# Eight of twelve modulation pieces moved from TensorE to ScalarE and GpSimd, with both layers written out

## The reference, cut to what matters

```python
for l in range(2):
    mod = einsum('bd,dk->bk', silu(c), w_ada[l]) + b_ada[l]          # 1024 x 6144 weights
    shift1, scale1, gate1, shift2, scale2, gate2 = split(mod, 6)
    h = rms_norm(x, norm1_g[l]) * (1 + scale1) + shift1
    proj = h @ w_in[l]                          # c_q 256, c_kv 128, k_rope 64, conv_u 1024
    attn_out = mla_group(...)                   # 4 heads, 512 x 512 scores
    conv_out = conv_group(conv_u, ...)          # gate, depthwise conv of 31 taps, norm, silu
    x = x + gate1 * (concat(attn_out, conv_out) @ w_out[l])
    h2 = rms_norm(x, norm2_g[l]) * (1 + scale2) + shift2
    x = x + gate2 * expert_choice_ffn(h2, ...)  # 16 experts, 64 tokens each, 12.6 MB of weights each
```

## Time and profile before

| | |
|---|---|
| median of three runs | 2568.12 us (2565.55 to 2569.09) |
| the profiled execution's own time | 2573.45 us |
| its span, first to last instruction | 2571.7 us |
| mean granted TensorE clock | 0.97 |
| TensorE busy | 2371.3 us, 92% |
| VectorE, ScalarE, GpSimd busy | 1126.1, 912.9, 268.7 us |
| layer 0, layer 1 start at (line 538) | 21.1, 795.6 us |
| key diagonal (line 1217) of layer 0, 1 | 161.3, 929.3 us |
| second block starts at about | 1558 us |

### The profile page before, as it was taken

One profiled execution on the slowest core, in us unless ns is written; L12 is line 12 of the kernel. 1 busy time (PEld: TensorE's weight loads), 2 busy tenths in 40 slices (PEclk: granted clock), 3 DMA queues, 4 the chain that ended last, 5 costly groups with the idle time before them and its releaser, 6 DMA issues. The chain is left out here.

```text
span 2571.7 us, 31324 instructions
## 1 busy us (share of the span) xinstructions
PE 2371.3 (92%) x12693; PEld 1495.2 (58%) x12693; DVE 1126.1 (44%) x1688; ACT 912.9 (35%) x1228; POOL 268.7 (10%) x245
## 2 busy tenths in 40 slices
PE   6998799998987999799999988999999999989997
PEld 5744544333335834534333437887888777767776
DVE  4976312211214975312111225647611112458997
ACT  4247211111114246211111116656632234247775
POOL 0000100000000000100000005000255433300100
PEclk8989899999998989899999999999999999989999
DMA  9801579999999601489999995422223421159995
GB/s 343 290 1 38 225 320 429 429 428 429 428 425 338 231 1 61 201 358 428 428 428 429 428 420 164 164 82 86 78 78 99 135 69 62 50 188 376 370 367 212
DMA packets 202868, 650.48 MB, mean 253 GB/s; under 512 B 12144, under 2 KB 110718, under 8 KB 177918
## 3 DMA queue, kind: packets, MB, share of 16 engines
q1 hardware_dynamic: 199028, 637.98, 63.7%
q0 software_dynamic: 2592, 7.87, 0.8%
q10 hardware_dynamic: 1130, 2.99, 0.3%
HBM read 641.99 MB, written 8.39 MB: 253 GB/s over the span
## 5 line engine op out<-in xcount | busy, mean ns | idle before, releaser
L847 PE MATMUL ps<-ring,hy 128*64 128x512 f32 x992 | 225.0, 595 | 37.1 <-DMA ring<-in_w_up 26.1
L1354 DVE TENSOR_TENSOR scr<-scr,ps 128x512 f32<-128x512 f32 x32 | 22.0, 688 | 504.2 <-PE ps L847 504.2
L847 PE MATMUL ps<-ring,scr 128*64 128x512 f32 x992 | 224.5, 594 | 16.8 <-DMA ring<-in_w_up 14.7
L1621 POOL TENSOR_TENSOR raw_r<-raw,w_high 128x512 fp32r<-128x512 f32 (+1 forms) x160 | 189.7, 1219 | 433.5 <-ACT w_high L1889 433.5
L874 PE MATMUL ps<-ring,scr 128*64 128x512 f32 x1024 | 227.2, 595 | 3.1 <-ACT scr L1064 2.7
L1644 PE MATMUL ps<-x_high,w_high 128*128 128x512 f32 x464 | 186.4, 402 | 3.6 <-DVE y L2285 3.6
L1646 PE MATMUL ps<-x_high,raw_r 128*128 128x512 f32 x464 | 184.5, 398 | 0.0
L1645 PE MATMUL ps<-xT_r,w_high 128*128 128x512 f32 x464 | 183.1, 395 | 0.0
L2710 DVE TENSOR_TENSOR ring_r<-ring,ring_high 128x2048 fp32r<-128x2048 f32 x77 | 172.8, 2285 | 22.0 <-ACT ring_high L2633 22.0
L847 PEld LDWEIGHTS ps<-ring,hy 128*64 128x64 f32 x992 | 68.4, 137 | 188.7 <-issue 123.4
L1141 DVE SCALAR_TENSOR_TENSOR one_hot_T<-h_tok,convw,one_hot_T 128x512 f32<-128x512 f32 x240 | 166.5, 749 | 1.8
(11 more groups left out here) (594 smaller groups left out, 4547.5 us busy)
## 6 DMA issues: line engine op xcount, KB each, us to landing
ring<-in_w_up SPq DMA_DIRECT2D x64, 2048.0 KB, 25.6
ring<-in_w_down SPq DMA_DIRECT2D x64, 2048.0 KB, 20.4
ring<-in_w_gate SPq DMA_DIRECT2D x60, 2048.0 KB, 23.0
ring<-in_w_up SPq DMA_DIRECT2D x56, 1024.0 KB, 6.9
ring<-in_w_ada SPq DMA_DIRECT2D x22, 2048.0 KB, 13.5
ring<-in_w_down SPq DMA_DIRECT2D x28, 1024.0 KB, 7.0
raw<-in_w_in SPq DMA_DIRECT2D x24, 1024.0 KB, 5.1
raw<-in_w_in SPq DMA_DIRECT2D x20, 512.0 KB, 5.2
```

What stands on the lines that cost most here:

```text
L847: mm = pe.matmul(ps[CAP * half:CAP * (half + 1), 1 + j // 2, :], x_e[j % 2][:, at_x:at_x + CAP], weights[:, k, half * HALF:(half + 1) * HA ...
L1621: part = pool.tensor_tensor(dst[:, a:a + 2], src[:, a:a + 2], high[:, a:a + 2].bitcast(F32), ALU.subtract)
```

## The change

- Pieces 5 to 12 (numbers 4 to 11) no longer go through TensorE's `ada_chunk`. Of the eight row tiles of a piece ScalarE scales the first four by the conditioning vector (`ada_scale`), GpSimd the other four; GpSimd then adds 2048, 1024 and 512 columns, and TensorE sums the 128 partitions of the result with four products of two columns (`ada_sums`). The pieces are taken in the order 6, 7, 8, 9, 4, 5, 10, 11. Loads of the later pieces and of the output weights wait for GpSimd's `ada_made`.
- The first four pieces are cut by rows (two row tiles, 2048 columns: runs of 8 KB), and go into four banks together.
- Both layers are written out; the branches on `l` become Python's.
- The 40 small products stand between the head products, their evacuation (`rbias`, `xmod`) behind the rotary parts.
- Taps: 68 behind tiles, 29 around the heads, 27 in attention. The convolution's mean, variance and normalization come three, three and two steps later.
- In the first pair of experts the first half is turned before the second half's gather ends, and the second half's turn and the gates come behind the first weight chunk.

Its core:

```diff
-TAPS_IN_TILE = (0, 5, 9, 9, 10, 10, 10, 10, 6, 1, 5, 4)
-TAPS_IN_HEADS = (16, 8)
-TAPS_IN_STEP = (3, 3, 2, 4, 3, 4, 2)
+TAPS_IN_TILE = (0, 5, 7, 8, 8, 8, 8, 8, 7, 1, 4, 4)
+TAPS_IN_HEADS = (20, 9)
+TAPS_IN_STEP = (3, 3, 3, 3, 3, 3, 3, 3, 3)
...
-ADA_PLACES = (0, 1, 2, 3, 0, 1, 2, 0, 1, 2, 0, 1)
+ADA_PLACES = (0, 1, 2, 3, 0, 1, 2, 1, 0, 1, 0, 1)
+ADA_CHUNK = (6, 7, 8, 9, 4, 5, 10, 11)
...
-    sp.dma_start(ada_place(M, c), w_ada[:, :, HALF * c:HALF * (c + 1)]).then_inc(ahead["ada"][c], 16)
+    sp.dma_start(first_rows(M, c), w_ada[:, 2 * c:2 * c + 2, 0:4 * HALF]).then_inc(ahead["ada"][c], 16)
+
+
+def first_rows(M, c):
+
+    return ada_place(M, c).rearrange("p k n -> p (k n)").rearrange("p (k n) -> p k n", k=2)
...
+    spare = ring[:, 2 * CHUNK - HALF:2 * CHUNK]
+    ada_acc = [spare, one_hot_T[:, 3 * KT * P:3 * KT * P + HALF]] * 2 + [spare, scr[:, 2, :], scr[:, 1, :], scr[:, 2, :]]
+    SUM_AT = [(6, 2 * P + 8 * k) for k in range(4)] + [(7, 2 * GROUP), (7, 2 * GROUP + 8), (7, 0), (7, 8)]
+    ada_row_all = one_hot_T[:, CHUNK:CHUNK + 4 * P].rearrange("p (c n) -> p c n", c=4)
...
                 before = max(b for b in range(c) if ADA_PLACES[b] == ADA_PLACES[c])
-                sp.wait_ge(ada_used, before + 1)
-                sp.dma_start(ada[c], w_ada[:, :, HALF * c:HALF * (c + 1)]).then_inc(ada_in[ADA_PLACES[c]], 16)
+                if before < 4:
+                    sp.wait_ge(ada_used, before + 1)
+                else:
+                    sp.wait_ge(ada_made, before - 3)
+                at_column = HALF * ADA_CHUNK[c - 4]
+                sp.dma_start(ada[c], w_ada[:, :, at_column:at_column + HALF]).then_inc(ada_in[ADA_PLACES[c]], 16)
...
-            for piece, then in ((2, (5,)), (CT, (6,)), (3, range(7, 12))):
+            for piece, then in ((2, (5,)), (CT, (6,)), (3, (7, 8))):
...
-            sp.wait_ge(ada_used, 12)
+            sp.wait_ge(ada_made, 3)
...
+            for c in range(9, 12):
+                ada_chunk(c)
             w = at("w_out").rearrange("a (k p) n -> p (a k) n", p=P)
             for k in range(0, KT, 4):
-                sp.dma_start(w_out[:, k:k + 4], w[:, k:k + 4]).then_inc(w_out_in, 16)
+                sp.wait_ge(ada_made, 7 + k // 4)
+                sp.dma_start(w_out[:, k:k + 4], w[:, k:k + 4]).then_inc(w_out_in[k // 4], 16)
...
+            step = Steps(pool, ada_step)
+            c_col = M["c_col"]
+            for k, acc_k in enumerate(ada_acc):
+                piece = ada[4 + k]
+                pool.wait_ge(ada_in[ADA_PLACES[4 + k]], ada_landed(4 + k, l))
+                for kt in range(4, KT):
+                    step(pool.tensor_scalar(piece[:, kt, :], piece[:, kt, :], c_col[:, kt:kt + 1], None, ALU.mult))
+                step.settle()
+                pool.wait_ge(ada_rows, k + 2)
+                step(pool.tensor_tensor(piece[:, 0:4, :], piece[:, 0:4, :], piece[:, 4:8, :], ALU.add))
+                step.settle()
+                step(pool.tensor_tensor(piece[:, 0:2, :], piece[:, 0:2, :], piece[:, 2:4, :], ALU.add))
+                step.settle()
+                if 2 <= k <= 4:
+                    pool.wait_ge(ada_cols, 4 + k - 1)
+                if k == 5:
+                    pool.wait_ge(lat_ss, 3)
+                if k == 7:
+                    pool.wait_ge(ada_cols, 4 + 6)
+                pool.tensor_tensor(acc_k, piece[:, 0, :], piece[:, 1, :], ALU.add).then_inc(ada_made, 1)
+
...
-            def ada_chunk(c, bank):
+            def ada_sums(k):
+                bank, col = SUM_AT[k]
+                pe.wait_ge(ada_made, k + 1)
+                for g in range(4):
+                    mm = pe.matmul(ps[:, bank, col + 2 * g:col + 2 * g + 2], ada_acc[k][:, g * P:(g + 1) * P], ones[:, 0:2], start=True, stop=True)
+                mm.then_inc(ada_cols, 1)
+
+            def ada_first(c):
                 pe.wait_ge(ada_in[ADA_PLACES[c]], ada_landed(c, l))
-                for kt in range(KT):
-                    for g in range(4):
-                        mm = pe.matmul(ps[GROUP * g:GROUP * (g + 1), bank, 0:P], c_rep[:, kt, :], ada[c][:, kt, g * P:(g + 1) * P],
-                                       start=(kt == 0), stop=(kt == KT - 1))
+                piece = first_rows(M, c)
+                for k in range(2):
+                    kt = 2 * c + k
+                    for n in range(4):
+                        for g in range(4):
+                            at_column = HALF * n + P * g
+                            mm = pe.matmul(ps[GROUP * g:GROUP * (g + 1), n, 0:P], c_rep[:, kt, :], piece[:, k, at_column:at_column + P],
+                                           start=(kt == 0), stop=(kt == KT - 1))
                 mm.then_inc(ada_used, 1)
 
             def ada_turn(c, bank):
...
-                c = 4 + at_tile
-                if 5 <= c <= 12:
-                    if c == 5:
-                        pe.wait_ge(n_xn, KT)
-                    if c == 9:
-                        pe.wait_ge(mod_ready, 2)
-                    ada_turn(c - 1, 7)
-                if c < 12:
-                    ada_chunk(c, 6)
+                if at_tile in (4, 6, 8, 9):
+                    ada_sums((4, 6, 8, 9).index(at_tile))
                 if at_tile == 9:
-                    pe.wait_ge(ada_rows, 12)
                     for k in range(3):
                         pe.wait_ge(lat_sq, k + 1)
                         grouped_sum(6, P * (k // 2), scr[:, k, :], k != 1, k != 0).then_inc(lat_ss, 1)
                 if at_tile == 10:
-                    pe.wait_ge(mod_ready, 3)
+                    pe.wait_ge(mod_ready, 2)
+                    pe.wait_ge(n_xn, KT)
...
+            def token_vectors(i):
+                for n, vector in enumerate((smod[:, KT:2 * KT], mod[:, SHIFT2:SHIFT2 + KT])):
+                    out = ps[GROUP * i:GROUP * (i + 1), 7, GROUP + KT * n:GROUP + KT * (n + 1)].rearrange("p (h k) -> p k h", h=2)
+                    for k in range(4):
+                        pe.matmul(out[:, k, :], every_fourth[:, k, :], vector.rearrange("p (h g) -> p g h", h=2)[:, i, :], start=True, stop=True)
+
+            def router_bias(kts):
+                for kt in kts:
+                    mm = pe.matmul(ps[:, 7, 0:GROUP], mod[:, SHIFT2 + kt:SHIFT2 + kt + 1].to_broadcast([P, P]), w_r[:, kt, :], start=(kt == 0), stop=(kt == KT - 1))
+                return mm
...
+                if i < 2:
+                    ada_sums(4 + i)
+                if i < TT:
+                    token_vectors(i)
+                elif i < 8:
+                    if i == TT:
+                        pe.wait_ge(pad_zero, 1)
+                    small = router_bias((2 * (i - TT), 2 * (i - TT) + 1))
+                    if i == 7:
+                        small.then_inc(r_bias_mm, 1)
...
+                if i in (2, 4):
+                    ada_sums(5 + i // 2)
+                if i == 10:
                     pe.wait_ge(conv_tap, CT * TAPS)
+                    pe.wait_ge(mod_ready, 3)
                     for c in range(CT):
...
+                    if first and r == 0 and j == 0:
+                        turn_half(0, 1)
+                        gates(0)
...
-            gather(0)
-            gates(0)
-            turn_tokens(0)
+            pe.wait_ge(s_built, 1)
+            gather_half(0, 0, range(TT)).then_inc(xe_mm, 1)
+            gather_half(0, 1, range(2))
+            turn_half(0, 0)
+            gather_half(0, 1, range(2, TT)).then_inc(xe_mm, 1)
...
+            act.wait_ge(ada_used, 4)
+            act.activation(ada_row_all, ps[:, 0:4, 0:P], ACT.Copy).then_inc(ada_rows, 1)
+            def ada_scale(k):
+                piece = ada[4 + k]
+                act.wait_ge(ada_in[ADA_PLACES[4 + k]], ada_landed(4 + k, l))
+                for kt in range(4):
+                    part = act.activation(piece[:, kt, :], piece[:, kt, :], ACT.Copy, scale=M["c_col"][:, kt:kt + 1])
+                part.then_inc(ada_rows, 1)
...
+                if at_tile in (1, 3, 5, 7, 10):
+                    ada_scale((0, 1, 3, 5, 7, 10).index(at_tile))
...
+                if i in (3, 9):
+                    ada_scale(6 if i == 3 else 7)
...
+            def modulation(at_mod, k, n):
+                bank, col = SUM_AT[k]
+                dve.wait_ge(ada_cols, 4 + k + n // 4)
+                return dve.tensor_tensor(mod[:, at_mod:at_mod + n], ps[:, bank, col:col + 2 * n].rearrange("p (n k) -> p n k", k=2)[:, :, 0],
+                                         vec[:, ADA + at_mod:ADA + at_mod + n], ALU.add)
...
-                if at_tile == 4:
-                    modulation(1).then_inc(mod_ready, 1)
-                if at_tile == 9:
-                    step(modulation(2))
-                    step.settle()
-                    dve.scalar_tensor_tensor(smod[:, KT:2 * KT], mod[:, SCALE2:SCALE2 + KT], 1.0, vec[:, N2G:N2G + KT], ALU.add, ALU.mult).then_inc(mod_ready, 1)
                 if at_tile == 10:
                     dve.wait_ge(lat_root, 2)
```

(5 more changed lines are left out.)

136 lines of the change are left out of this document (60 added, 76 removed).

## The result

The changed kernel takes **2667.82 us** (median of 4 runs, 2664.61 to 2668.88) against 2568.09 us (4 runs of the kernel before): ratio 1.0381, 95% interval 1.0368 to 1.0394, slower by 3.8%. The profiled execution took 2668.43 us (span 2666.7). The forecast was 2649 us in a range of 2590 to 2705, slower with a chance of 0.83: the side holds, and so does the main mechanism (GpSimd's additions shut VectorE out), and the centre is 19 us short.

A forecast was written before the change was run, and what follows sets the result against it. TensorE and VectorE were taken to fill the input-tile window, the DMA stream to bound the experts. Layers +94, first pieces -4, written-out layers -5, first pair -4: +81 us, 2649 us on the median's scale; range 2590 to 2705.

The forecast's parts named there:

- Modulation: Input-tile window: 82 us of GpSimd work a layer, 56 of it added to VectorE; window 148 instead of 99.7, +48.
- the price of a scaling: GpSimd's scaling of 512 columns: 0.52 us, half a 1024-column copy; upper end 1.26, from a two-input subtraction.
- a scaling blocks for its whole time: Input tiles: any GpSimd instruction, scalings too, excludes VectorE's two-SBUF-input taps and low halves throughout; seen at a 0.97 us instruction.
- Taps and normalization: Six taps leave the input window (-4.1 us a layer) for attention (+4); later normalization nothing, 2 us without cover.
- Small products: Small products moved from before the key factor to between head products: -5 us a layer.
- in their new place ScalarE limits the head products: Head products: ScalarE sets their pace, so small products between them were taken to cost TensorE nothing; basis of -5 a layer.
- First pair: Start of expert stage: first weight chunk free 2 us earlier, so the bounding stream starts then; -2 a layer, -4.
- Layers written out: Layer boundary: TensorE's 5.49 us standstill shortened; -5 us once, ends 0 and -10.
- First pieces: Layer 0's first modulation loads as whole rows: 8.4 MB at 428 instead of 343 GB/s; -4 us, ends 0 and -5.
- the exclusion costs nothing: Rival, input window: GpSimd runs beside the taps unhindered, -9 us a layer and -13; 2537 us, 14%.
- scalings at the price of two inputs: Rival, GpSimd's pieces: each scaling 0.74 us dearer, 32 times a layer, +48; 2697 us, 15%.
- VectorE wins the turns: Rival, input tiles: GpSimd works only where taps stop, TensorE waits for late `ada_made`; 8 us a layer less, 2633 us, 10%.

The follow-up runs named there:

- vectors_late: Kernel before with layers written out, whole-row first pieces and token vectors moved into TensorE's wait for the ranks: 2547.85 us, ratio 0.9920.
- others_only: Kernel before with every part of the change but the modulation; pieces 5 to 12 stay on TensorE, taps and convolution steps as before: 2556.04 us, ratio 0.9943.
- no_scalings: Changed kernel without GpSimd's four scalings of each piece, its additions kept: 2649.09 us, ratio 1.0317 to the kernel before.

## Why the prediction was right, and where it was not

Over the whole kernel, by medians (each difference is good to some 3 to 5 us):

- **Modulation.** On record 2 x (48 + 4.1) = 104 us apart from the taps moved out; measured 2667.82 - 2563.51 = 104. The size is right and its working is not: two wrong steps nearly cancelled, which is luck. The step that failed is the price of a scaling: 0.52 us was taken from a copy, whose row was no guide, and both ends (0.52, 1.26) lay below the 1.95 us measured. The second step that failed is that a scaling blocks for its whole time, read from a 0.97 us instruction beside a copy: the copy does, the scaling does for some 0.4 of its 1.8 us. 32 scalings of 1.95 us that cost 0.17 of their time are 10.6 us; 32 of 0.52 that cost all of it would be 16.6. The additions carry the rest, and their rows were the right ones. In place, too, it differs: 42 and 45 us a layer fall before the key factors (169.0 for 126.8, 169.1 for 124.4). Of the rest, 4 and 6 us a layer fall in the attention, as the difference of 98.0 to 93.9 us and 96.0 to 89.8 from the key factors to the first update of x shows; what is left of the 102 us between the spans, some 5, falls into code that both share (3.0 us behind layer 1, 1.0 and 1.2 ahead of the two modulation vectors).
- **Taps and normalization.** On record -4.1 in the window, +4 in attention, nothing for the normalization, with 2 us if its cover failed. Measured +7.5 in all: the window gained nothing (TensorE was as full there as VectorE, as the earlier trace rows said), and the normalization's cover failed: the SiLUs came 1 us later behind the last score reduction in each layer, half of what the record named for this case. The rest is 1.9 us of shared code and the slower score steps of layer 0, at a lower granted clock.
- **Small products.** -10 on record, 0 measured. The step that failed is "in their new place ScalarE limits the head products": there were no gaps between them, before or after. vectors_late shows, in layer 0, where part of a gain lay: in the clock behind them, which the prediction read in the earlier trace rows and counted as nothing.
- **First pair.** -4 on record, 0 measured: the step "the stream that bounds the stage starts then" failed: in the first pair TensorE is full and has no wait on a DMA, and the early bytes are lost again within 88 us; a share of DMA time over 440 us hid that.
- **Layers written out.** -5 on record with an end at -10; measured -8.9, -10.5 by the ratio. The gap's row was read, and what the pause does to the clock of the first piece behind it was not.
- **First pieces.** -4 on record; 3.3 us at best in a trace, and 3.7 are left of others_only's 12.5 when the 8.9 of the layers written out are taken off. The term was right; its working was not: the rate from 10 to 42 us rose from 357 to 382 GB/s, not to the 428 that the term was built on. By the rule of the Trainium skill (DMA: Bandwidth & Descriptors, "Specifications") of 358 GB/s the term would be 0; the trace moves 382 beside 357, so the measurement decides against it again.

On record the sum was +81 us, measured is +99.7 (2667.82 - 2568.09). The errors of the terms in the order above, 0, +7.7, +10, +4, -3.9 and +0.3, make 18.2 of these 18.7. That they add up is no test: the modulation's and the taps' terms are differences of the same few kernels, and the last term is what others_only leaves.

Of the rivals, "the exclusion costs nothing" is refuted by taps of 1.22 us; "scalings at the price of two inputs" was nearest in GpSimd's busy time and wrong in its effect; "VectorE wins the turns" is refuted as the cause of the time by TensorE's waits, none of which is on `ada_made`.

## What to carry to other kernels

Additions moved to GpSimd were charged to VectorE here, at 0.78 of their time, wherever VectorE read two SBUF tensors: count such work as VectorE's own, and measure one instruction of the very form first, since a scaling was slower alone and yet cost its neighbour less. A pause or a run of tiny products on TensorE was followed by a lower clock here (0.50 behind the 5.49 us gap, 0.57 over the 64 products' end and what follows), so the place to try for them is ahead of a wait that is there anyway. A stage that is bound by its stream on average can be bound by TensorE at its start, and a head start of the stream is then worth nothing.

## What was not expected of the hardware

- GpSimd's `tensor_scalar` on 128 x 512 float32 takes 1.49 to 1.57 us alone, its two-input addition of the same size 1.04 us.
- A GpSimd instruction that reads SBUF doesn't always shut a VectorE one with two SBUF inputs out for its whole time. The Trainium skill (SBUF — State Buffer, "Who interferes with whom") calls it an exclusive lock, and names no operation of GpSimd that is exempt. Beside additions this case agrees (one tap per addition, 4.98 us behind one of 4.60), beside scalings it does not (taps of 1.17 and 0.74 us in turn beside scalings of 1.78). The measurement decides; why the scaling lets VectorE in was not found.
- It works the other way too: VectorE can hold a GpSimd instruction off for many instructions in a row. GpSimd's addition of 2048 columns takes 6.07 us on average in no_scalings and 4.70 in the changed kernel, since one of the eight takes 13.21 us.
